# Last expert pairs in another order, the last w2 by column halves, and the final norm by halves on three engines

## The chip, the cores and the metric

The kernel runs on one core of one Trainium2 chip. The core has five engines with queues of their own: TensorE (PE), VectorE (DVE), ScalarE (ACT), GpSimd (POOL) and SyncE (SP), which here only issues transfers. They meet at semaphores. The metric is the device time of one execution in microseconds (us), the median of several runs.

## The reference, cut to what matters

One block of a hybrid encoder over 512 tokens of width 1024 in f32: two kinds of attention, cross attention to 256 memory tokens, then a mixture of 32 experts in 4 groups, of which every token takes two, and a last norm. The change touches the experts and the last norm:

```python
def expert_block(args):
    tok, gte, e = args
    xb = x_pad[tok]
    hb = jax.nn.silu(xb @ w1[e]) * (xb @ w3[e])
    return (hb @ w2[e]) * gte[:, None].astype(x2.dtype)
...
y = jnp.zeros((n + 1, d), x2.dtype).at[slot_tok].add(y_slots.reshape(n_slots, d))
...
h = h + y_f.reshape(b, s, d)
return rms_norm(h, final_norm)      # h / sqrt(mean(h*h) + 1e-6) * final_norm
```

w1 and w3 are (1024, 512) for each expert and w2 is (512, 1024).

## The kernel before, in words

The first half of the kernel does norms, projections and attention. From about 540 us on it works through the 32 experts in 16 pairs (`NPAIR`), p = 0 to 15. Each expert has a block of up to 64 tokens (`BLK`), so a pair fills 128 rows. What more tokens an expert has is done by loops at the end (`n_over`); the trace has no row of them, so these inputs do not need them.

For a pair, G = x w1 and U = x w3 are summed in two PSUM banks, ScalarE forms sigmoid(G) (`sg`), VectorE gg = G sg and then Hs = gg · gate · U. TensorE transposes Hs (`turn_hidden`), ScalarE copies the result out of PSUM to `HT` (`hidden`), and TensorE forms Y = H w2 in PSUM banks 4 and 5, 512 columns each (`down`). ScalarE copies Y to `Yh` (`output`), VectorE keeps the rest, `Yl` = Y - Yh (`rest`), and TensorE brings the rows of the pair back to their tokens by products with a 0/1 matrix `S` (`combine`, eight tiles of 128 tokens x 512 columns, two products each). VectorE adds these eight tiles to `h` (`add_one`).

Weights come as parts c of an expert: 0 and 1 are the halves of w1, 2 and 3 of w3, 4 and 5 of w2, 1 MB each. `SEQ_W` is the order in which TensorE uses them; a load is issued by SP when the place that it takes, one of nine in the ring `eraw`, was used (`e_wused`). `take_place` builds the list `LOADS` from that order. So the order of the loads and the order of the products come from one table. In it G of a pair stands ahead of w2 of the pair before: while TensorE does G of pair p, VectorE and ScalarE make Hs and HT of pair p-1.

The last pair has its own forms: `last_up` does U in two column halves (banks `U_BANK`), so that Hs, the transposes (`turn_last`) and HT (`last_hidden`) go by halves too; its w2 rows are laid out so that part 4 needs only the first half of HT. Both parts cover all 1024 columns. The sums of pair 14 are cut in two (`combine_half`), one ahead of U's second half and one between the two last transposes.

The last norm: ScalarE forms the sum of squares of each of four token tiles (128 x 1024), VectorE from these the inverse root (`inverse_root`: mean, ScalarE's square root, one over it, and one Newton step) for tiles 0 and 1, then for 2 and 3 (`step`). Tiles 0, 2 and 3 are scaled by VectorE in one product with the root and `gain_o`, tile 1 (`OUT_ACT`) by ScalarE (root) and GpSimd (gain). SP stores tiles in the order 0, 2, 1, 3.

Of the kernel before, what the change touches and what calls it, by code (L numbers as in the profile page):

```python
# [6 lines left out]
D = 1024  # L7
# [3 lines left out]
TT = SEQ // P  # L11
# [10 lines left out]
NE = NG * EPG  # L22
DE = 512
BLK = 64
# [17 lines left out]
def build(nc, x, mem, mix_norm, w_in, lam_q1, lam_k1, lam_q2, lam_k2, diff_subln, w_branch_a, w_branch_b,  # L42
# [486 lines left out]
    over_read = sem("over_read")  # L529
    u_half, out_by_root, out_rooted, out_done = (sem(n) for n in ("u_half", "out_by_root", "out_rooted", "out_done"))  # L530
# [62 lines left out]
    def take_place(parts):  # L593

        slot = took[0] % NS
        took[0] += 1
        for e, c, n, start in parts:
            free_at = max([LAST_OF.get((slot, start + WCH * i), 0) for i in range(n)])
            LOADS.append((slot, start, e, c, n, free_at))
# [25 lines left out]
    LAST_COMB = [(0, 0), (1, 0), (0, 1), (1, 1), (2, 0), (2, 1), (3, 0), (3, 1)]  # L625
# [3 lines left out]
    OUT_ACT = 1  # L629
    LAST_BANK = [6, 3, 1, 2, 0, 7, 4, 5]  # L630
# [27 lines left out]
    def place_view(slot, start, c, n):  # L658
        return eraw[slot][:, start:start + WCH * n].rearrange("p (k n) -> p k n", n=512 if c < 4 else D)

    block = nc.Block()
    with block:
# [3 lines left out]
        def _(sp):  # L666
# [17 lines left out]
            def load_expert(n):  # L684
                slot, start, e, c, halves, _ = LOADS[n]
                sp.dma_start(place_view(slot, start, c, halves), expert_src(e, c, halves)).then_inc(e_loaded[slot], 16)
# [69 lines left out]
        def _(pool):  # L756
# [82 lines left out]
            pool.wait_ge(out_rooted, 2)  # L839
            pool.wait_ge(out_by_root, 1)  # L840
            pool.tensor_tensor(h[:, OUT_ACT, :], h[:, OUT_ACT, :], gain_o[:, :], ALU.mult).then_inc(out_scaled[OUT_ACT], 1)


        @block.scalar
        def _(act):
# [261 lines left out]
            def output(p):  # L1107

                if p:
                    act.wait_ge(comb_made, NC * p)  # L1110
                for n in (0, 1):
                    if n == 0:
                        act.wait_ge(y_half, p + 1)
                    else:
                        act.wait_ge(e_wused, both_used(p, 5))
                    act.activation(Yh[:, 512 * n:512 * n + 512], ps[4 + n][:, :], ACT.Copy).then_inc(yh_kept, 1)  # L1116

            rows_kept(0)
            for p in range(NPAIR):
                if p:  # L1120
                    hidden(p - 1)
                act.wait_ge(e_wused, both_used(p, 1))
# [3 lines left out]
                if p:  # L1126
                    output(p - 1)
# [32 lines left out]
            act.activation(sqr[:, 15:16], ident[:, 0:1], ACT.Sqrt)  # L1160
            for t in range(TT):
                act.wait_ge(comb_added, NC * (NPAIR - 1) + LAST_COMB.index((t, 1)) + 1)
                act.wait_ge(n_sum, SUM_UPTO["h2"] + t)
                act.activation(junk_t[:, :], h[:, t, :], ACT.Square, accum_out=ss[:, t:t + 1]).then_inc(n_sum, 1)
                if t % 2 == 1:
                    root("out", slice(t - 1, t + 1), t // 2)

            act.wait_ge(out_rooted, 1)
            act.activation(h[:, OUT_ACT, :], h[:, OUT_ACT, :], ACT.Copy, scale=rs[:, OUT_ACT:OUT_ACT + 1]).then_inc(out_by_root, 1)
# [3 lines left out]
        def _(dve):  # L1173
# [395 lines left out]
            def body(p):  # L1569

                dve.wait_ge(sg_done, p + 1)
                dve.tensor_tensor(gg[:, :], ps[1][:, :], sg[:, :], ALU.mult).then_inc(gg_done, 1)  # L1572
                if p:
                    rest(p - 1)
                if p + 1 < NPAIR:
                    rows_kept(p + 1)
                if p:
                    add_half(p - 1, 0)
                    if p + 1 < NPAIR:
                        add_half(p - 1, 1)  # L1580
# [16 lines left out]
                if p == NPAIR - 1:  # L1597
                    add_half(p - 1, 1)
# [67 lines left out]
            for step in (0, 1):  # L1666
                dve.wait_ge(n_sum, SUM_UPTO["h2"] + 2 * step + 2)
# [9 lines left out]
        def _(pe):  # L1677
# [360 lines left out]

            def turn_last(half):
# [15 lines left out]
            def down(p, c):  # L2055
# [3 lines left out]
                pe.wait_ge(ht_kept, p + 2 if (p, c) == (NPAIR - 1, 5) else p + 1)  # L2059
                if c == 4 and p:  # L2060
                    pe.wait_ge(comb_added, NC * p if p < NPAIR - 1 else NC * p - NC // 2)
# [27 lines left out]
            def body(p):  # L2089
                pe.wait_ge(xt_kept, 2 * p + 2)  # L2090
                if p:
# [22 lines left out]
                if p < NPAIR - 1:  # L2114
                    up(p, 2)
                else:
                    last_up(2)
                if p:
                    combine_half(p - 1, 0)
                if p == NPAIR - 1:  # L2120
                    last_up(3)
                    turn_last(0)

                    pe.wait_ge(gg_done, p + 1)
                    combine_half(p - 1, 1)
                    turn_last(1)
                    return
# [13 lines left out]
            down(NPAIR - 1, 4)  # L2141
            down(NPAIR - 1, 5)
# [72 lines left out]
```

## Time and profile before

| | us |
|---|---|
| median of 3 runs | 1037.38 (1037.16 to 1037.48) |
| the profiled execution | 1035.97 |
| its span | 1034.2 |
| TensorE busy | 986.9 (95%) |
| VectorE busy | 502.9 (49%) |
| ScalarE busy | 341.8 (33%) |
| GpSimd busy | 42.9 (4%) |
| expert weights (`eraw`), share of the last chain | 12% |

Times in the rows are counted from the start of the span. In the part with the experts TensorE is busy for 90% or more of nearly every slice of the page, and so are the DMA engines, which move 425 to 430 GB/s there. A row of the timeline or the chain puts like instructions together (x16 is sixteen of them); a product with f32 operands counts as two. In brackets stands the engine's idle time before it, and what ended it.

### The profile page before, as it was taken

The page shows a single profiled execution, that of the slowest core. Times are in us where ns is not written, and L with a number is a line of the kernel's source. Part 1 is how long each engine was busy: PE and PEld are TensorE (multiplying, and loading weights), DVE is VectorE, ACT ScalarE, POOL GpSimd, SP SyncE. Part 2 cuts the span into 40 slices and gives each one's busy share as a digit, 9 for nine tenths or more (in the row PEclk, how much of TensorE's full clock was granted, in tenths as well). Part 3 has the DMA queues.
Part 4 walks back from the last instruction along what each step waited for, and adds up shares of the span by engine and source line. Part 5 has one row for each costly group of instructions (what it writes and reads, how often), then busy time and mean ns, then how long its engine had stood idle before and what let it go on. Part 6 is the DMA issues. An engine that isn't in the chain of part 4 may idle for free.

```text
span 1034.2 us, 12625 instructions
## 1 busy us (share of the span) xinstructions
PE 986.9 (95%) x4909; PEld 624.6 (60%) x4909; DVE 502.9 (49%) x920; ACT 341.8 (33%) x685; POOL 42.9 (4%) x62
## 2 busy tenths in 40 slices
PE   8999999999999999999996999999999889898994
PEld 6778877867788898877785344444443333333342
DVE  5369799777466355433338133333332223333336
ACT  6332356767862354534233111111111110111113
POOL 1000000000000000000001000000000000000001
PEclk9999999999999999999998999999999999999998
DMA  8422222121123535313297999999999999999992
GB/s 237 136 82 82 90 74 82 41 82 42 42 82 135 192 122 174 125 69 122 65 389 293 408 430 424 427 427 425 428 425 427 429 427 426 427 425 425 420 415 113
DMA packets 65583, 260.72 MB, mean 252 GB/s; under 512 B 11457, under 2 KB 39154, under 8 KB 50930
## 3 DMA queue, kind: packets, MB, share of 16 engines
q1 hardware_dynamic: 61106, 248.08, 60.4%
q0 software_dynamic: 3392, 8.39, 2.2%
q10 hardware_dynamic: 1024, 3.41, 0.9%
q8 instruction: 41, 0.67, 0.3%
q14 instruction: 20, 0.16, 0.0%
HBM read 259.60 MB, written 4.19 MB: 255 GB/s over the span
## 4 chain that ended last, share of the span: by engine, by line
PE 74%; DMA 13%; DVE 5%; ACT 3%; issue 3%; DVEq 0%; ACTq 0%; SPq 0%; POOLq 0%
PE ps L2014 16%; PE ps L1694 12%; DMA eraw<-in_w 12%; PE ps L1696 12%; PE ps L1695 12%; PE ps L2067 8%; PE ps L2078 2%; PE ps L2079 2%; PE ps L1929 1%; PE ps L1951 1%; PE ps L1871 1%; PE ps L2001 1%; DVE s L1306 1%; DVE nmax L1308 1%; PE ps L2052 1%
## 5 line engine op out<-in xcount | busy, mean ns | idle before, releaser
L2014 PE MATMUL ps<-eraw,XT 128*64 128x512 f32 x992 | 226.0, 598 | 10.8 <-DMA eraw<-in_w 9.6
L1257 DVE TENSOR_TENSOR wlo<-raw,whi 128x2048 fp32r<-128x2048 f32 (+2 forms) x43 | 95.9, 2230 | 117.3 <-ACT whi L939 117.2
L2014 PEld LDWEIGHTS ps<-eraw,XT 128*64 128x64 f32 x992 | 67.2, 136 | 131.9 <-issue 127.6
L2067 PE MATMUL ps<-eraw,HT 128*64 128x512 f32 x512 | 112.9, 593 | 7.8 <-issue 7.8
L1563 DVE TENSOR_TENSOR h<-ps,h 128x512 f32<-128x512 f32 x128 | 79.4, 684 | 81.6 <-PE ps L2079 81.6
L1694 PE MATMUL ps<-xT_hi,whi 128*128 128x512 f32 (+1 forms) x256 | 103.8, 405 | 1.3 <-DVE xT_lo L1264 1.3
L1696 PE MATMUL ps<-xT_hi,wlo 128*128 128x512 f32 (+1 forms) x256 | 100.2, 392 | 0.0
L1695 PE MATMUL ps<-xT_lo,whi 128*128 128x512 f32 (+1 forms) x256 | 100.0, 391 | 0.0
L939 ACT ACTIVATE whi<-raw 128x2048 fp32r<-128x2048 f32 (+2 forms) x43 | 80.2, 1866 | 45.4 <-PE ps L1696 45.4
L2067 PEld LDWEIGHTS ps<-eraw,HT 128*64 128x64 f32 x512 | 38.7, 137 | 79.8 <-issue 79.2
L1097 ACT ACTIVATE HT<-ps 128x512 f32<-128x512 f32 x15 | 9.0, 597 | 195.7 <-PE ps L2052 195.7
L1555 DVE TENSOR_TENSOR Yl<-ps,Yh 128x512 fp32r<-128x512 f32 x32 | 22.1, 692 | 96.2 <-ACT Yh L1116 96.2
L1694 PEld LDWEIGHTS ps<-xT_hi,whi 128*128 128x128 f32 (+1 forms) x256 | 47.7, 186 | 20.2 <-issue 8.9
L1572 DVE TENSOR_TENSOR gg<-ps,sg 128x512 f32<-128x512 f32 x16 | 11.1, 692 | 96.5 <-ACT sg L1125 94.5
L1696 PEld LDWEIGHTS ps<-xT_hi,wlo 128*128 128x128 f32 (+1 forms) x256 | 47.7, 186 | 10.9
L2078 PE MATMUL ps<-Yh,S 128*128 128x512 f32 x128 | 53.7, 419 | 0.4 <-issue 0.4
L1695 PEld LDWEIGHTS ps<-xT_lo,whi 128*128 128x128 f32 (+1 forms) x256 | 47.8, 187 | 9.4
L1116 ACT ACTIVATE Yh<-ps 128x512 fp32r<-128x512 f32 x32 | 19.1, 597 | 100.2 <-PE ps L2067 100.2
L2079 PE MATMUL ps<-Yl,S 128*128 128x512 f32 x128 | 50.4, 394 | 0.0
L2078 PEld LDWEIGHTS ps<-Yh,S 128*128 128x128 f32 x128 | 24.0, 187 | 28.9 <-issue 24.4
L1011 ACT ACTIVATE s<-s,nmax 128x128 f32<-128x128 f32 (+3 forms) x64 | 35.4, 559 | 1.1 <-DVE nmax L1308 1.0
L1125 ACT ACTIVATE sg<-ps 128x512 f32<-128x512 f32 x16 | 9.6, 597 | 77.0 <-PE ps L2014 77.0
(325 smaller groups left out, 1563.4 us busy)
## 6 DMA issues: line engine op xcount, KB each, us to landing
eraw<-in_w SPq DMA_DIRECT2D x74, 2048.0 KB, 27.7
eraw<-in_w SPq DMA_DIRECT2D x44, 1024.0 KB, 25.8
raw<-in_w_in SPq DMA_DIRECT2D x9, 1024.0 KB, 5.0
raw<-in_w_gate SPq DMA_DIRECT2D x8, 1024.0 KB, 5.4
raw<-in_w_ckv SPq DMA_DIRECT2D x8, 1024.0 KB, 5.3
raw<-in_w_out SPq DMA_DIRECT2D x4, 1024.0 KB, 5.1
raw<-in_w_cq SPq DMA_DIRECT2D x4, 1024.0 KB, 5.0
raw<-in_w_co SPq DMA_DIRECT2D x4, 1024.0 KB, 5.0
```

The lines of the kernel that those rows point to most:

```text
L939: act.activation(whi[n % 2][:, 0:w], raw[n % RING][:, 0:w], ACT.Copy).then_inc(w_hi, 1)
L1011: act.activation(b, b, ACT.Exp, bias=nmax[:, u % 3, m:m + 1], accum_out=ssum[:, u % 3, m:m + 1]).then_inc(exp_done, 1)
L1257: dve.tensor_tensor(wlo[n % 2][:, 0:w], raw[n % RING][:, 0:w], whi[n % 2][:, 0:w].bitcast(f32), ALU.subtract).then_inc(w_lo, 1)
L1555: dve.tensor_tensor(Yl[:, c], ps[4 + n][:, :], Yh[:, c].bitcast(f32), ALU.subtract).then_inc(yl_kept, 1)
L1563: dve.tensor_tensor(v, ps[bank][:, :], v, ALU.add).then_inc(comb_added, 1)
L1694: pe.matmul(o, ahi, bhi, start=start, stop=False)
L1695: pe.matmul(o, ahi, blo, start=False, stop=False)
L1696: return pe.matmul(o, alo, bhi, start=False, stop=stop)
L2014: ins = pe.matmul(ps[1 + c // 2][rows, :], XT[p % 2][:, kk, rows], eraw[slot][:, first + 512 * k:first + 512 * k + 512], start=(kk == 0), ...
L2067: ins = pe.matmul(ps[4 + n][rows, :], HT[:, ff, rows], eraw[slot][:, first + D * f + 512 * n:first + D * f + 512 * n + 512], start=(ff == ...
L2078: pe.matmul(o, S[:, P * t:P * t + P], Yh[:, c], start=True, stop=False)
L2079: pe.matmul(o, S[:, P * t:P * t + P], Yl[:, c], start=False, stop=True).then_inc(comb_made, 1)
```

## The change

It has three parts.

1. In `SEQ_W`, and in the code of TensorE, ScalarE and VectorE, w2 of pair 14 comes ahead of G of pair 15. Both halves of the sums of pair 14 now stand ahead of U's second half, and the two last transposes directly behind it.
2. w2 of the last pair is loaded and used by column halves: part 4 is columns 0 to 511 of all 512 rows and part 5 columns 512 to 1023, the latter in two pieces of two row groups with a semaphore for each. Rows of 4 KB in the load become rows of 2 KB. `last_down` replaces `down` for this pair.
3. The eight last tiles are summed in the order of their columns (first 0 to 511 of all tokens, `LAST_COMB`). Each addition is followed by a square of that half on ScalarE; VectorE adds the two sums. Of every tile VectorE scales columns 512 to 1023, while columns 0 to 511 are multiplied by the gain on GpSimd, as soon as their squares are taken, and then by the root on ScalarE. Stores go in the order 0 to 3.

```diff
-        for q, c in ((p, 0), (p, 1), (p - 1, 4), (p - 1, 5), (p, 2), (p, 3)):
+        ahead, behind = [(p, 0), (p, 1)], [(p - 1, 4), (p - 1, 5)]
+        for q, c in (behind + ahead if p == NPAIR - 1 else ahead + behind) + [(p, 2), (p, 3)]:
...
-    def take_place(parts):
+    def take_place(parts, pieces=(None,)):
...
-                take_place([(e, c + half, 1, 0), (e + 1, c + half, 1, WCH)])
+                take_place([(e, c + half, 1, 0), (e + 1, c + half, 1, WCH)],
+                           [slice(0, 2), slice(2, 4)] if (e, c + half) == (NE - 2, 5) else [None])
...
-    LAST_COMB = [(0, 0), (1, 0), (0, 1), (1, 1), (2, 0), (2, 1), (3, 0), (3, 1)]
+    LAST_COMB = [(t, n) for n in (0, 1) for t in range(TT)]
...
-            v = w2v_last
+            return w2v_last[e, :, :, 512 * (c - 4):512 * (c - 4) + 512]
...
 sync:
-            for t in (0, 2, 1, 3):
-                sp.wait_ge(out_scaled[t], 1)
+            for t in range(TT):
+                sp.wait_ge(out_scaled[t], 2)
...
 gpsimd:
-            pool.wait_ge(out_rooted, 2)
-            pool.wait_ge(out_by_root, 1)
-            pool.tensor_tensor(h[:, OUT_ACT, :], h[:, OUT_ACT, :], gain_o[:, :], ALU.mult).then_inc(out_scaled[OUT_ACT], 1)
+            for t in range(TT):
+                pool.wait_ge(out_sum, t + 1)
+                pool.tensor_tensor(h[:, t, 0:512], h[:, t, 0:512], gain_o[:, 0:512], ALU.mult).then_inc(gained, 1)
...
 scalar:
+            for j, (t, n) in enumerate(LAST_COMB):
+                act.wait_ge(comb_added, NC * (NPAIR - 1) + j + 1)
+                if j >= 2:
+                    act.wait_ge(out_sum, j - 1)
+                act.activation(junk_t[:, 512 * (j % 2):512 * (j % 2) + 512], h[:, t, 512 * n:512 * n + 512], ACT.Square,
+                               accum_out=ss[:, TT * n + t:TT * n + t + 1]).then_inc(out_sum, 1)
+                if j == NC - 2:
+                    root("out", slice(0, 2), 0)
+            root("out", slice(2, 4), 1)
+
             for t in range(TT):
...
+                act.wait_ge(out_rooted, t // 2 + 1)
+                act.wait_ge(gained, t + 1)
+                act.activation(h[:, t, 0:512], h[:, t, 0:512], ACT.Copy, scale=rs[:, t:t + 1]).then_inc(out_scaled[t], 1)
...
 vector:
+                if name == "out":
+                    link(dve.tensor_tensor(ss[:, c], ss[:, c], ss[:, TT + c.start:TT + c.stop], ALU.add))
...
                 for t in (2 * step, 2 * step + 1):
-                    if t != OUT_ACT:
-                        dve.scalar_tensor_tensor(h[:, t, :], h[:, t, :], rs[:, t:t + 1], gain_o[:, :],
-                                                 ALU.mult, ALU.mult).then_inc(out_scaled[t], 1)
+                    dve.scalar_tensor_tensor(h[:, t, 512:], h[:, t, 512:], rs[:, t:t + 1], gain_o[:, 512:],
+                                             ALU.mult, ALU.mult).then_inc(out_scaled[t], 1)
...
 tensor:
+            def last_down(n):
+                p = NPAIR - 1
+                at_ = [PLACE[2 * p + m, 4 + n] for m in (0, 1)]
+                pe.wait_ge(comb_added, NC * p - NC // 2)
+                for ff in range(4):
+                    if n == 0 and ff == 0:
+                        for slot, _, upto in at_:
+                            pe.wait_ge(e_loaded[slot], upto)
+                    elif n == 1 and ff % 2 == 0:
+                        pe.wait_ge(last_loaded[ff // 2], 32)
+                    pe.wait_ge(ht_kept, p + 1 + ff // 2)
+                    for m, (slot, first, _) in enumerate(at_):
...
             def body(p):
                 pe.wait_ge(xt_kept, 2 * p + 2)
+                if p == NPAIR - 1:
+                    turn_hidden(p - 1)
+                    down(p - 1, 4)
+                    down(p - 1, 5)
+                    pe.wait_ge(gg_done, p)
+                    up(p, 0)
+                    up(p, 1)
+                    combine_half(p - 1, 0)
+                    last_up(2)
+                    pe.wait_ge(gg_done, p + 1)
+                    combine_half(p - 1, 1)
+                    last_up(3)
+                    turn_last(0)
+                    turn_last(1)
+                    return
```

On TensorE, where pair 14 meets pair 15, the order before was (XT_110 are the tokens of pair 14 and XT_111 those of pair 15; eraw_62 to eraw_64 and eraw_56 to eraw_59 are places of the ring; `ident,Hs` are transposes, `eraw,HT` is w2; this list counts a product once):

```order
L2014 MATMUL ps<-eraw_62,XT_110 64x512 x4
L2014 MATMUL ps<-eraw_63,XT_111 64x512 x4
L2052 MATMUL ps<-ident,Hs 128x128 x4
L2014 MATMUL ps<-eraw_63,XT_111 64x512 x4
L2014 MATMUL ps<-eraw_64,XT_111 64x512 x8
L2067 MATMUL ps<-eraw_56,HT 64x512 x8
L2067 MATMUL ps<-eraw_57,HT 64x512 x8
L2031 MATMUL ps<-eraw_58,XT_111 64x256 x16
L2078 MATMUL ps<-Yh,S 128x512
```

and it is now, in the same place:

```order
L2031 MATMUL ps<-eraw_62,XT_110 64x512 x4
L2087 MATMUL ps<-ident,Hs 128x128 x4
L2102 MATMUL ps<-eraw_63,HT 64x512 x8
L2102 MATMUL ps<-eraw_64,HT 64x512 x8
L2031 MATMUL ps<-eraw_56,XT_111 64x512 x8
L2031 MATMUL ps<-eraw_57,XT_111 64x512 x8
L2113 MATMUL ps<-Yh,S 128x512
L2114 MATMUL ps<-Yl,S 128x512
```

The transposes moved from the middle of G to directly behind the last product of pair 14's U, w2 moved ahead of G, and the first half of the sums moved from behind U's first half to directly behind G.

On TensorE behind U's second half of the last pair the order before was:

```order
L2031 MATMUL ps<-eraw_59,XT_111 64x256 x16
L2043 MATMUL ps<-ident,Hs 128x128 x2
L2078 MATMUL ps<-Yh,S 128x512
L2079 MATMUL ps<-Yl,S 128x512
L2078 MATMUL ps<-Yh,S 128x512
L2079 MATMUL ps<-Yl,S 128x512
L2078 MATMUL ps<-Yh,S 128x512
L2079 MATMUL ps<-Yl,S 128x512
L2078 MATMUL ps<-Yh,S 128x512
L2079 MATMUL ps<-Yl,S 128x512
L2043 MATMUL ps<-ident,Hs 128x128 x2
L2140 TENSOR_LOAD over_i
```

and now it is (`eraw_60` and `eraw_61` hold the two parts of the last w2):

```order
L2113 MATMUL ps<-Yh,S 128x512
L2114 MATMUL ps<-Yl,S 128x512
L2048 MATMUL ps<-eraw_59,XT_111 64x256 x16
L2078 MATMUL ps<-ident,Hs 128x128 x4
L2179 TENSOR_LOAD over_i
L2179 ISA x2
L2069 MATMUL ps<-eraw_60,HT 64x512 x8
L2069 MATMUL ps<-eraw_61,HT 64x512 x8
```

The sums no longer stand between the two pairs of transposes.

On ScalarE the end of the kernel was (`ss` are the sums of squares, `sqr<-vv` the square roots):

```order
L1160 ACT_TABLE_LOAD
L1160 ACTIVATE sqr<-ident 128x1
L1164 ACTIVATE junk_t,ss<-h 128x1024 x2
L861 ACTIVATE sqr<-vv 128x2
L1164 ACTIVATE junk_t,ss<-h 128x1024 x2
L861 ACTIVATE sqr<-vv 128x2
L1169 ACTIVATE h<-h,rs 128x1024
```

and is now:

```order
L1172 ACT_TABLE_LOAD
L1172 ACTIVATE sqr<-ident 128x1
L1177 ACTIVATE junk_t,ss<-h 128x512 x7
L869 ACTIVATE sqr<-vv 128x2
L1177 ACTIVATE junk_t,ss<-h 128x512
L869 ACTIVATE sqr<-vv 128x2
L1186 ACTIVATE h<-h,rs 128x512 x4
```

Both roots stand ahead of all four scalings.

## Rows read from the trace of the kernel before

**Rows 1.** The chain that ended last, in order of time: start us, us, what
```profile
970.38 26.66 DMA eraw<-in_w
...
1027.67 3.28 DVEq L662
```

**Rows 2.** Windows: busy PE, PEld, DVE, ACT, POOL; PEclk, DMA share, GB/s
```profile
970.40:996.40 26.00, 26.00 (x118) 9.95 (x116) 9.24 (x15) 2.93 (x7) 0.00 (x0) 1.00 1.01 422
```

**Rows 3.** Timeline, last pairs: start us, us, engine, line, op, [idle before]
```profile
979.99 3.65 PE L2014 MATMUL ps<-eraw,XT 128*64 128x512 f32 x16
...
982.09 0.75 DVE L1586 SCALAR_TENSOR_TENSOR Hs<-gg,pair_gates,ps 128x512 f32<-128x512 f32 x1 [0.89 <-PE ps L2014]
...
983.57 0.75 PE L2052 MATMUL ps<-ident,Hs 128*128 128x128 f32 x4
...
984.36 0.60 ACT L1097 ACTIVATE HT<-ps 128x512 f32<-128x512 f32 x1 [12.66 <-PE ps L2052]
...
989.45 7.04 PE L2067 MATMUL ps<-eraw,HT 128*64 128x512 f32 x32
...
997.18 3.67 PE L2031 MATMUL ps<-eraw,XT 128*64 128x256 f32 x32 [0.69 <-DMA eraw<-in_w]
...
1006.42 0.44 PE L2043 MATMUL ps<-ident,Hs 128*128 128x128 f32 x2
1006.57 0.48 DVE L1595 SCALAR_TENSOR_TENSOR Hs<-gg,pair_gates,ps 128x256 f32<-128x256 f32 x1 [1.17 <-PE ps L2031]
1006.62 0.48 PE L2078 MATMUL ps<-Yh,S 128*128 128x512 f32 x1
...
1008.55 0.38 PE L2043 MATMUL ps<-ident,Hs 128*128 128x128 f32 x2
1008.87 7.09 PE L2067 MATMUL ps<-eraw,HT 128*64 128x512 f32 x32
```

**Rows 4.** Line L686, the last load alone: issue, and time to landing
```profile
L686 SPq DMA_DIRECT2D eraw<-in_w x1: 4312/4312/4312, 990.3 to 990.3; - x1
...
DMA to landing us min/median/max: 21.9/21.9/21.9
```

**Rows 5.** Windows: a w_out load, last w2 loads, last stores
```profile
294.50:295.00 0.50, 0.50 (x4) 0.42 (x3) 0.00 (x0) 0.50 (x2) 0.00 (x0) 1.00 1.05 410
1004.00:1005.00 1.00, 1.00 (x12) 0.67 (x10) 0.13 (x2) 0.00 (x0) 0.00 (x0) 1.00 1.03 410
1032.00:1032.50 0.50, 0.00 (x0) 0.00 (x0) 0.00 (x0) 0.00 (x0) 0.00 (x0) 0.50 1.01 410
```

**Rows 6.** Timeline behind the last products, VectorE and ScalarE
```profile
1017.33 4.88 DVE L1563 TENSOR_TENSOR h<-ps,h 128x512 f32<-128x512 f32 x8
...
1017.93 0.20 ACT L1160 ACTIVATE sqr<-ident 128x1 f32<-128x1 f32 x1
...
1022.12 0.16 DVE L1200 TENSOR_SCALAR vv<-ss 128x2 f32<-128x2 f32 x1
...
1022.55 0.17 DVE L1202 RECIPROCAL rs<-sqr 128x2 f32<-128x2 f32 x1 [0.27 <-ACT sqr L861]
...
1023.65 1.28 DVE L1672 SCALAR_TENSOR_TENSOR h<-h,rs,gain_o 128x1024 f32<-128x1024 f32 x1
```

**Rows 7.** Timeline of ScalarE, two exponentials with a running sum
```profile
270.44 0.71 ACT L1011 ACTIVATE s<-s,nmax 128x512 f32<-128x512 f32 x1
...
271.14 0.71 ACT L1011 ACTIVATE s<-s,nmax 128x512 f32<-128x512 f32 x1
```

**Rows 8.** Line L1672, its three products: count, durations ns, first and last start
```profile
L1672 DVE SCALAR_TENSOR_TENSOR h<-h,rs,gain_o x3: 1283/1284/3360, 1023.7 to 1027.6; 128x1024 f32<-128x1024 f32 x3
```

**Rows 9.** Timeline of GpSimd's product in the tail
```profile
1026.44 3.42 POOL L841 TENSOR_TENSOR h<-h,gain_o 128x1024 f32<-128x1024 f32 x1 [83.34 <-DVEq L1669]
```

**Rows 10.** Line L751, the four stores: issues, and time to landing
```profile
L751 SPq DMA_DIRECT2D out<-h x4: 332/344/369, 1025.0 to 1031.0; - x4
...
DMA to landing us min/median/max: 2.6/2.6/2.8
```

More of the change, by code:

```diff
@@ L529, in build @@
     over_read = sem("over_read")
+    last_loaded = [sem(f"last_loaded{i}") for i in (0, 1)]
+    out_sum, gained = sem("out_sum"), sem("gained")
     u_half, out_by_root, out_rooted, out_done = (sem(n) for n in ("u_half", "out_by_root", "out_rooted", "out_done"))
@@ L591, in build @@
     took = [0]
-    def take_place(parts):
+    def take_place(parts, pieces=(None,)):
         slot = took[0] % NS
         took[0] += 1
-        for e, c, n, start in parts:
-            free_at = max([LAST_OF.get((slot, start + WCH * i), 0) for i in range(n)])
-            LOADS.append((slot, start, e, c, n, free_at))
+        for rows in pieces:
+            for e, c, n, start in parts:
+                free_at = max([LAST_OF.get((slot, start + WCH * i), 0) for i in range(n)])
+                LOADS.append((slot, start, e, c, n, rows, free_at))
         upto = 16 * sum(load[0] == slot for load in LOADS)
@@ L656, in hidden_tile, with place_view @@
         return slice(P * ff, P * ff + P) if p == NPAIR - 1 else slice(ff, DE, 4)
-    def place_view(slot, start, c, n):
-        return eraw[slot][:, start:start + WCH * n].rearrange("p (k n) -> p k n", n=512 if c < 4 else D)
+    def place_view(slot, start, c, n, by_columns=False):
+        return eraw[slot][:, start:start + WCH * n].rearrange("p (k n) -> p k n", n=512 if c < 4 or by_columns else D)
     block = nc.Block()
@@ L684, in load_expert @@
             def load_expert(n):
-                slot, start, e, c, halves, _ = LOADS[n]
-                sp.dma_start(place_view(slot, start, c, halves), expert_src(e, c, halves)).then_inc(e_loaded[slot], 16)
+                slot, start, e, c, halves, rows, _ = LOADS[n]
+                last_w2 = c >= 4 and e // 2 == NPAIR - 1
+                dst, src = place_view(slot, start, c, halves, last_w2), expert_src(e, c, halves)
+                if rows is not None:
+                    dst, src = dst[:, rows], src[:, rows]
+                sp.dma_start(dst, src).then_inc(last_loaded[rows.start // 2] if last_w2 and c == 5 else e_loaded[slot], 16)
             def load_place(slot):
@@ L1111, in output @@
                 for n in (0, 1):
-                    if n == 0:
+                    if p == NPAIR - 1:
+                        act.wait_ge(e_wused, both_used(p, 4 + n))
+                    elif n == 0:
                         act.wait_ge(y_half, p + 1)
@@ L1121, in _ @@
                     hidden(p - 1)
+                if p == NPAIR - 1:
+                    output(p - 1)
                 act.wait_ge(e_wused, both_used(p, 1))
@@ L1125, in _ @@
                 act.activation(sg[:, :], ps[1][:, :], ACT.Sigmoid).then_inc(sg_done, 1)
-                if p:
+                if 0 < p < NPAIR - 1:
                     output(p - 1)
@@ L1160, in _ @@
             act.activation(sqr[:, 15:16], ident[:, 0:1], ACT.Sqrt)
-            for t in range(TT):
[L1162 to L1169, printed above, removed]
+            for j, (t, n) in enumerate(LAST_COMB):
[7 more added lines that the diff above has]
+            root("out", slice(2, 4), 1)
+            for t in range(TT):
+                act.wait_ge(out_rooted, t // 2 + 1)
+                act.wait_ge(gained, t + 1)
+                act.activation(h[:, t, 0:512], h[:, t, 0:512], ACT.Copy, scale=rs[:, t:t + 1]).then_inc(out_scaled[t], 1)
         @block.vector
@@ L1569, in body @@
             def body(p):
+                if p == NPAIR - 1:
+                    rest(p - 1)
                 dve.wait_ge(sg_done, p + 1)
                 dve.tensor_tensor(gg[:, :], ps[1][:, :], sg[:, :], ALU.mult).then_inc(gg_done, 1)
-                if p:
+                if 0 < p < NPAIR - 1:
                     rest(p - 1)
@@ L1578, in body @@
                     add_half(p - 1, 0)
-                    if p + 1 < NPAIR:
-                        add_half(p - 1, 1)
+                    add_half(p - 1, 1)
                 dve.wait_ge(gg_done, p + 1)
@@ L1666, in _ @@
             for step in (0, 1):
-                dve.wait_ge(n_sum, SUM_UPTO["h2"] + 2 * step + 2)
+                dve.wait_ge(out_sum, NC // 2 + 2 * step + 2)
                 inverse_root("out", D, slice(2 * step, 2 * step + 2), step)
@@ L2037, in last_up @@
                                 ins.then_inc(u_half, 1)
+            def last_down(n):
[10 more added lines that the diff above has]
+                    for m, (slot, first, _) in enumerate(at_):
+                        rows = slice(BLK * m, BLK * m + BLK)
+                        ins = pe.matmul(ps[4 + n][rows, :], HT[:, ff, rows], eraw[slot][:, first + 512 * ff:first + 512 * ff + 512],
+                                        start=(ff == 0), stop=(ff == 3))
+                        if ff == 3:
+                            ins.then_inc(e_wused, 1)
             def turn_last(half):
@@ L2058, in down @@
                     pe.wait_ge(e_loaded[slot], upto)
-                pe.wait_ge(ht_kept, p + 2 if (p, c) == (NPAIR - 1, 5) else p + 1)
+                pe.wait_ge(ht_kept, p + 1)
                 if c == 4 and p:
-                    pe.wait_ge(comb_added, NC * p if p < NPAIR - 1 else NC * p - NC // 2)
+                    pe.wait_ge(comb_added, NC * p)
                 for n, f in [(0, 0), (1, 0), (0, 1), (1, 1)] if c == 4 else [(0, 0), (0, 1), (1, 0), (1, 1)]:
@@ L2090, in body @@
                 pe.wait_ge(xt_kept, 2 * p + 2)
+                if p == NPAIR - 1:
+                    turn_hidden(p - 1)
[12 more added lines that the diff above has]
+                    return
                 if p:
@@ L2113, in body @@
                     pe.wait_ge(h_done, p)
[L2114 to L2117, printed above, removed]
+                up(p, 2)
                 if p:
                     combine_half(p - 1, 0)
[L2120 to L2127, printed above, removed]
                 up(p, 3, (0, 1))
@@ L2140, in _ @@
             n_over = pe.value_load(over_i[0:1, 0:1], min_val=0, max_val=MAX_OVER)
-            down(NPAIR - 1, 4)
-            down(NPAIR - 1, 5)
+            last_down(0)
+            last_down(1)
             with pe.If(n_over > 0):
```

5 lines of the change are left out of this document (1 added, 4 removed).

## The prediction, written before the run

> **What bounds the kernel now.** I read the chain of waits from its end first. Its last long wait for data is a piece 26.66 us long that starts at 970.38 and ends at 997.04 [rows 1]: the first half of U's weights (w3) of the last pair of experts. Before it the stream of expert weights sets the pace, and behind it no transfer stands in the chain. Next I asked what TensorE did meanwhile. The windows show it busy for 26.00 of 26.00 us from 970.4 to 996.4, at a granted clock of 1.00, with the DMA engines full too, at 422 GB/s [rows 2]. So in the last 26 us before that wait both are full, and the wait that names the DMA cost TensorE 0.69 us, no more [rows 3]. That is the point of my argument: the stream can be rearranged, but the work of TensorE behind it has no slack. Then I read the order of TensorE's work for the last two pairs in the timeline [rows 3]. Sixteen pieces start at 979.99 (the trace counts each product as two); eight of them end U of pair 14, the other eight begin G of pair 15. While these run, VectorE makes Hs from 982.09 to 982.84, so the transposes at 983.57 find it ready, and while ScalarE copies HT (984.36, 0.60 us) TensorE goes on with G. No product waits. w2 of pair 14 follows at 989.45, U of pair 15 at 997.18, and w2 of pair 15 from 1008.87 for 7.09 us, to 1015.96. I call that end E; the span's end at 1034.2 is E+18.24. The last load lands at 990.3 + 21.9 = 1012.2 [rows 4].
>
> The profiled execution took 1035.97 us, its span 1034.2, so 1.8 us lie around it. The median of the timed runs is 1037.38, 1.4 us above the profiled one. I work the change out within the span and add it to the median.
>
> **The last pairs, part by part.** Nothing changes before the end of U of pair 14, eight pieces into the group at 979.99, at 979.99 + (983.57 - 979.99)/2 = 981.78. The loads are issued behind the same waits, and each pair of loads takes the place that another one had.
> - The idle time of 0.69 us before 997.18 goes. U's first half now starts behind G and one half of the sums of pair 14, about 1000.5 (984.35 below, plus 7.05 for w2, 7.16 for G's 32 pieces at the same pace, and 2.0 for the sums), when its weights have been there since 997.04. That is -0.69.
> - The transposes of pair 14 now stand right behind the last product that Hs needs. Hs starts at 982.09 and takes 0.75, the transposes can start at 982.9, HT starts 0.79 behind them as now (983.57 to 984.36), ends at 984.3, and w2 starts at 984.35. From 981.78 that is 2.57 us, of which the transposes are 0.7: TensorE idles for 1.87 that G of pair 15 now covers. From below, Hs and HT could not be quicker than their 0.75 and 0.60, so 1.4 is the least; 2.3 if each handover costs 0.1 more. I take +1.87.
> - The second half of the sums moves ahead of U's second half, so that nothing covers the last transposes. Now 2.45 us lie between the first of them (1006.42) and w2 (1008.87), 1.93 of them sums (1006.62 to 1008.55). Then the second Hs (starts 0.15 behind, takes 0.48) lets the second transposes start at 0.65, and w2 starts 0.32 later (1008.55 to 1008.87), at 0.97; the sums cost their 1.93, and some 0.1 of a fresh start, elsewhere. 0.97 + 2.03 - 2.45 = +0.55; at least +0.3.
> - w2 of the last pair by column halves has the same 32 pieces, 7.09 us. The halves of its last data are wanted when its columns 512 to 1023 start, some 3.5 us before the new end, and 1.8 before it. With the new end near 1017.7 these are 1014.1 and 1015.9, against 1012.2 now. The rows of 4 KB become 2 KB: the stream's rate with 4 KB rows is 410 GB/s, and a load of w_out, which has 2 KB rows, also runs at 410 [rows 5]. Were it 5% less, the last 4 MB would be 0.5 us late, and 1.9 us of slack hide that. SP's two additional DMAs wait behind a full queue, but the next thing SP waits for comes ten microseconds later. I cost this at nothing, gain included: the first half of Y is ready early, but TensorE has no place to use it before its last product.
>
> Sum for TensorE: -0.69 + 1.87 + 0.55 = +1.73. The new end E is 1017.7.
>
> **Sums, squares and scaling.** All counted from E. The first addition starts at E+1.37 and eight take 4.88, to E+6.25, as now [rows 6]; the order of the columns does not change that.
> - The squares start when the square root's table is in, at E+2.2 (1017.93 + 0.20). Two exponentials of 512 columns with a running sum follow each other in 0.70 us (270.44, 271.14) [rows 7]; six squares at 0.70 are read out by E+6.4 to 6.5. So they keep up with the additions.
> - GpSimd now multiplies four halves while VectorE adds. The one multiplication of 1024 columns is recorded at 3.42 us, but VectorE's product started at the same time as it took its usual 1.28, and the next one took 3.36 [rows 8, 9]. So they took turns: GpSimd held VectorE up for 3.36 - 1.28 = 2.08. Half of it is 1.04 a half tile; 1.71 from the recorded span is the upper bound. Four from E+3.0 end at E+7.2 (at most E+9.8). The new addition of two sums on VectorE would start at E+6.5; it reads SBUF twice, as the held-up product did, and I let it wait until E+7.2. The Trainium skill, page "SBUF — State Buffer", section "🔬 SBUF: two separate sides", says that a VectorE operation with two SBUF inputs and a GpSimd operation that reads SBUF exclude each other for the whole instruction. By that rule the trace agrees (3.36 against 1.28), and the running additions, with one input in PSUM, would not be held.
> - Then ss ready E+7.4, mean E+7.56 (0.16 each), root E+7.8, Newton's steps 1.10 (1022.55 to 1023.65), so scaling starts at E+8.95. Two half tiles take 1.4 (0.75 for one of 512, some 0.65 behind another) to E+10.35. Only then does VectorE form the second mean, 0.43 (1022.12 to 1022.55) plus 0.2 for the sum: E+10.98.
> - ScalarE is held by its own order: its second root stands ahead of all its scalings. So tiles 0 and 1 are scaled at E+11.0 to 12.15 (0.60 each), tiles 2 and 3 by E+12.75 and 13.4. The first store goes at E+11.6. It now goes at 1025.0, which is E+9.0.
> - Four stores of 512 KB then follow within 1.9 us. One lands 2.6 us after its issue [rows 10]; at 410 GB/s its bytes are 1.28 of that. Four one behind the other: 2.6 - 1.28 + 5.12 = 6.44 after the first issue, E+18.05. Behind the last landing (1031.0 + 2.8 = 1033.8) stand 0.4 us now: E+18.45. Now it is E+18.24, so this part gives +0.2 at my values. Squares at 0.63 or an addition that isn't held give -0.7; GpSimd at 1.71 gives +2.6 at most. The stall of 2.08 in VectorE's last product goes, and 1.3 us of stores that now lie ahead of the others come to lie behind them.
>
> Total +1.73 + 0.2 = +1.9: 1037.38 + 1.9 = 1039.3.
>
> **Rivals.**
> 1. The additions are held by GpSimd too. No row shows a GpSimd operation that reads SBUF beside an addition out of PSUM. If each of the four multiplications takes a turn of 1.04 from E+3.2 on, the eighth addition ends at E+10.4, not 6.25, and the mean starts there instead of at E+7.2: 3.2 more, +5.1, 1042.5. It decides from the second turn on, since one turn is hidden behind the squares. Against it: the rule above. Chance 12%.
> 2. The stream, not TensorE, sets the end. Then w2 ends 1.77 (eight of its 32 pieces) behind the last landing, 1012.2 + 1.77 = 1014.0, not 1017.7: 1014.0 is 1.96 before 1015.96, and with +0.2 that gives 1035.6, or 1034.7 with the second part at its -0.7. For it: the chain names the DMA up to 997.04. Against it: 26.00 of 26.00 us busy. Chance 7%. It would be on the fast side, and only just.
> 3. The stores do not queue behind each other, so the last one alone counts: E+13.4 + 0.1 + 2.8 + 0.4 = E+16.7, 1.5 less than now; +1.73 - 1.5 gives 1037.6. Against it: the stores alone reach the 410 GB/s that the weights reach too [rows 5], so each fills all the engines. Chance 5%.
>
> **The numbers.** My forecast holds 76%, at 1037.9 to 1040.6: TensorE's terms can be 0.5 less (bubble 1.4, last transposes 0.3) or 0.4 more, the second part -0.7 to +0.9 before the extremes. About 0.2%, 2.07 us, is what a measurement can tell from no change; the forecast of +1.9 lies just inside. So I give it 42% of its weight as slower and 58% within: 0.32 and 0.44. Rival 1 adds 0.12 to slower, rival 2 gives 0.05 to faster and 0.02 to within, rival 3 0.05 to within. Together faster 0.05, within 0.51, slower 0.44. The range reaches towards rival 2 and up to rival 1: 1036.4 to 1042.4.
>
> **What would show it.** TensorE idle for about 1 us on each side of the transposes at 983, w2 of pair 14 at 984.4, no wait for eraw behind 981, its last product at 1017.7. U's first half starting at 1000.5. If w2 of pair 14 starts before 983.7, or the last product ends before 1016.5, my sum is wrong in its first part. VectorE's additions still 0.61 apart; if 1.6 apart, rival 1. The addition of ss between E+6.5 and E+7.4. ScalarE's first scaling behind its second root, near E+11; the four stores issued within 2 us. A first store before E+10 would make the second part wrong.

## The result, and the profile after

| | before, us | after, us |
|---|---|---|
| median | 1037.43 (8 runs, 1036.56 to 1038.06) | 1041.91 (8 runs, 1038.89 to 1042.78) |
| profiled execution / its span | 1035.97 / 1034.2 | 1042.65 / 1040.9 |
| A, start of the last eight pieces of U of pair 14 | 979.99 | 981.80 |
| E, end of w2 of pair 15 | 1015.96 (A+35.97) | 1022.10 (A+40.30) |
| span's end | E+18.24 | E+18.80 |

After takes 1.0042 of the time of before, interval 1.0033 to 1.0052: +4.5 us, slower. The predicted +1.9 was on the right side of nothing, and too small by more than half. That A itself lies 1.81 later does not come from the change: the seven kernels with the new order had A from 979.42 to 981.80, the five with the old one from 979.99 to 981.85, and up to A they all do the same work. What differs is TensorE's granted clock much earlier: in a pause of 5.7 us at 548 it falls to 0.50 in every trace, and stays there for 6.8 us in before and for 10.2 us in after. So I count from A to E and from E to the end: +4.33 and +0.56.

TensorE's rows of after for the last two pairs (the timeline; columns as in [rows 3]), with the two copies and Hs:

```profile
981.80 1.94 PE L2031 MATMUL ps<-eraw,XT 128*64 128x512 f32 x8
...
983.91 0.75 DVE L1606 SCALAR_TENSOR_TENSOR Hs<-gg,pair_gates,ps 128x512 f32<-128x512 f32 x1 [0.89 <-PE ps L2031]
...
984.75 0.72 PE L2087 MATMUL ps<-ident,Hs 128*128 128x128 f32 x4 [1.02 <-issue]
...
985.51 0.60 ACT L1105 ACTIVATE HT<-ps 128x512 f32<-128x512 f32 x1 [12.00 <-PE ps L2087]
...
986.37 8.78 PE L2102 MATMUL ps<-eraw,HT 128*64 128x512 f32 x32 [0.89 <-ACT HT L1105]
...
994.95 7.06 PE L2031 MATMUL ps<-eraw,XT 128*64 128x512 f32 x32
...
1004.01 3.67 PE L2048 MATMUL ps<-eraw,XT 128*64 128x256 f32 x32
...
1009.66 3.67 PE L2048 MATMUL ps<-eraw,XT 128*64 128x256 f32 x32
...
1013.26 0.44 PE L2078 MATMUL ps<-ident,Hs 128*128 128x128 f32 x2
...
1013.94 0.44 PE L2078 MATMUL ps<-ident,Hs 128*128 128x128 f32 x2 [0.24 <-DVE Hs L1615]
1014.32 0.75 DVE L1567 SCALAR_TENSOR_TENSOR S<-slot_row,pair_slots,S 128x512 fp32r<-128x512 f32 x1
1014.42 0.38 ACT L1111 ACTIVATE HT<-ps 128x256 f32<-128x256 f32 x1 [0.29 <-PE ps L2078]
```

The transposes have a gap on each side, 1.02 and 0.89, where [rows 3] has none. And w2 of pair 14, 32 pieces as before, takes 8.78 where it took 7.04. The windows of after say why (busy of TensorE, PEclk, DMA share, GB/s):

```profile
985.00:986.00 1.00, 0.48 (x4) 1.00 1.02 426
986.00:987.00 1.00, 0.64 (x2) 0.77 1.00 418
987.00:988.00 1.00, 1.00 (x5) 0.50 0.98 410
988.00:989.00 1.00, 1.00 (x6) 0.50 1.02 426
989.00:990.00 1.00, 1.00 (x5) 0.53 1.02 426
990.00:991.00 1.00, 1.00 (x6) 1.00 1.02 426
```

For 3.4 us (986.5 to 989.9, by the shares in the windows) TensorE runs at a granted clock of 0.50, its 1.2 GHz level, just as w2 begins, and then it is back at 1.00, 2.4 GHz. It takes windows of a microsecond or two to see this; a slice of the page's clock row is 26 us long.

TensorE's waits of after, from 981 to 1023 (total, times, longest), name no transfer; in [rows 3] one stood there:

```profile
PE ps L2087 <- issue: 1.0, 1, 1.0
PE ps L2102 <- ACT HT L1105: 0.9, 1, 0.9
PE ps L2069 <- ACT HT L1111: 0.6, 1, 0.6
PE ps L2078 <- DVE Hs L1615: 0.2, 1, 0.2
```

The tail of after, VectorE, ScalarE and GpSimd:

```profile
1023.45 4.88 DVE L1582 TENSOR_TENSOR h<-ps,h 128x512 f32<-128x512 f32 x8
...
1024.17 0.63 ACT L1177 ACTIVATE junk_t<-h 128x512 f32<-128x512 f32 x1
...
1024.80 0.62 ACT L1177 ACTIVATE junk_t<-h 128x512 f32<-128x512 f32 x1
1024.98 4.97 POOL L849 TENSOR_TENSOR h<-h,gain_o 128x512 f32<-128x512 f32 x4 [80.67 <-ACT junk_t L1177]
...
1028.24 0.51 DVE L1218 TENSOR_TENSOR ss<-ss 128x2 f32<-128x2 f32 x1
...
1028.78 1.20 DVE L1219 TENSOR_SCALAR vv<-ss 128x2 f32<-128x2 f32 x1
...
1031.35 1.41 DVE L1689 SCALAR_TENSOR_TENSOR h<-h,rs,gain_o 128x512 f32<-128x512 f32 x2
...
1033.18 2.54 ACT L1186 ACTIVATE h<-h,rs 128x512 f32<-128x512 f32 x4
```

The additions are where they were, E+1.35 for 4.88 [rows 6], though GpSimd works beside them. The mean (`vv`), two columns wide, takes 1.20 where [rows 6] has 0.16. The stores by their line, to be read against [rows 10]:

```profile
L759 SPq DMA_DIRECT2D out<-h x4: 356/384/980, 1033.9 to 1035.9; - x4
...
DMA to landing us min/median/max: 2.7/3.7/4.6
```

They are issued within 2.0 us and take from 2.7 up to 4.6 us to land, where [rows 10] has 2.6 to 2.8: they queue.

### The profile page after: what moved, and what is told of

Same layout as the page of the kernel before. It is cut to its first block, busy times and chain, and to the rows that moved or that the text cites. A ratio compares the mean times of both kernels' runs of the same rounds, so it can differ in the third digit from the quotient of the medians.

```text
span 1040.9 us, 12648 instructions
## 1 busy us (share of the span) xinstructions
PE 990.6 (95%) x4909; PEld 627.1 (60%) x4909; DVE 501.5 (48%) x923; ACT 343.8 (33%) x696; POOL 44.5 (4%) x65
## 4 chain that ended last, share of the span: by engine, by line
PE 82%; DMA 10%; ACT 3%; DVE 2%; issue 2%; ACTq 0%; DVEq 0%
PE ps L2031 17%; PE ps L1711 13%; PE ps L1713 13%; PE ps L1712 13%; DMA eraw<-in_w 9%; PE ps L2102 8%; PE ps L2113 3%; PE ps L2114 2%; PE ps L1888 2%; PE ps L1946 1%; PE ps L1968 1%; PE ps L2018 1%; PE ps L1896 1%; PE ps L1909 1%; PE ps L2087 1%
## 5 line engine op out<-in xcount | busy, mean ns | idle before, releaser
L2102 PE MATMUL ps<-eraw,HT 128*64 128x512 f32 x480 | 107.6, 601 | 8.8 <-issue 7.8
```

The lines of the kernel that those rows point to most:

```text
L2102: ins = pe.matmul(ps[4 + n][rows, :], HT[:, ff, rows], eraw[slot][:, first + D * f + 512 * n:first + D * f + 512 * n + 512], start=(ff == ...
```

## The experiments

Each was compared with the kernel before in runs on the same chip. My theory at this point: after is slower by the order of the last pairs (two gaps, and the clock that they cost), a little by the norm, and not at all by the column halves. The rival: each part costs some, or the columns and their 2 KB rows slow the stream.

**The order alone.** The changes to `SEQ_W` and to the code of TensorE, ScalarE and VectorE for pair 14, nothing else:

```diff
+            if p == NPAIR - 1:
+                turn_hidden(p - 1)
+                down(p - 1, 4)
+                down(p - 1, 5)
```

> Only the first part: w2 of pair 14 ahead of G of pair 15, both halves of pair 14's sums ahead of U's second half, the last transposes together; last w2 and the norm as before. Theory (TensorE's order is the cost): TensorE stands for 1.0 us on either side of pair 14's transposes, its granted clock then falls to half for some 3.5 us and w2 of pair 14 takes 8.8 instead of 7.05, and the last w2 starts 1 us later behind the last transposes; +3.5 to +4.6 us against before. Rival (the stream or the norm is the cost): under +1.5 us.

Measured: 1040.49 (6 runs) against 1036.52, ratio 1.0031 (1.0019 to 1.0043). A to E is 40.28, +4.31, the tail 18.28. Both gaps and the slow w2 are there:

```profile
983.80 0.72 PE L2056 MATMUL ps<-ident,Hs 128*128 128x128 f32 x4 [1.02 <-issue]
...
985.41 8.78 PE L2071 MATMUL ps<-eraw,HT 128*64 128x512 f32 x32 [0.89 <-ACT HT L1100]
```

So the order holds all of TensorE's loss, and some nine tenths of the whole in the traces.

**The norm alone.** `LAST_COMB`, the squares and scalings by halves, and the stores' order:

```diff
-    LAST_COMB = [(0, 0), (1, 0), (0, 1), (1, 1), (2, 0), (2, 1), (3, 0), (3, 1)]
+    LAST_COMB = [(t, n) for n in (0, 1) for t in range(TT)]
```

> Only the third part: sums, squares and scaling by halves on three engines; the order and the last w2 as before. Theory: the end of TensorE stays, and behind it 18.8 us instead of 18.24, because the second mean waits for GpSimd's fourth product and the four stores go within 2 us; +0.3 to +0.9 us. Rival (the additions or the norm carry the loss): +2 us or more, additions of VectorE over 0.61 us apart.

Measured: 1037.12 (12 runs) against 1036.52, ratio 1.0002 (0.9994 to 1.0011). In the trace the tail is 18.79, +0.55, the same as in after; that is less than the timing can tell from nothing.

**The column halves alone.** `last_down` for the last pair, and its loads:

```diff
-            down(NPAIR - 1, 4)
-            down(NPAIR - 1, 5)
+            last_down(0)
+            last_down(1)
```

> Only the second part: the last w2 loaded and used by column halves, in rows of 2 KB; the order and the norm as before. Theory: nothing, -0.3 to +0.4 us, since TensorE uses each half later than it lands. Rival (2 KB rows slow the stream): the last loads land 1 us or more later and w2's second half waits, +1 us or more.

Measured: 1036.73 (11 runs) against 1036.52, ratio 0.9999 (0.9990 to 1.0008); A to E 35.98, tail 18.26. Nothing, as costed. The 2 KB rows cost the end nothing.

**Is it the gaps that cost the clock?** After, with useless products of 128x256 put in both, four ahead of pair 14's transposes and three behind:

```diff
+                    for _ in range(4):
+                        pe.matmul(ps[7][:, 0:256], ident[:, :], gain_o[:, 0:256], start=True, stop=True)
                     turn_hidden(p - 1)
+                    for _ in range(3):
+                        pe.matmul(ps[7][:, 0:256], ident[:, :], gain_o[:, 0:256], start=True, stop=True)
```

> The changed kernel with seven products without use (128x256, to an idle bank) in the two gaps at pair 14's transposes, four ahead of them and three behind. Theory (the idle time lowers the granted clock): the clock stays 1.00 there, w2 of pair 14 takes 7.05 us instead of 8.8, the gaps themselves stay 1.0 and 0.9 us long; 1.2 to 2.0 us faster than the changed kernel, +2.5 to +3.3 against before. Rival (w2 is slowed by something else, its data or its copy): no change against the changed kernel, +4.5.

Measured: 1040.97 (6 runs), ratio 1.0040 (1.0027 to 1.0054). The clock is 1.00 from 980 to 992 and w2 takes 7.09, but it starts at A+5.56 and not A+4.57: a filler takes 0.46 there, in all a microsecond more than the gaps held. A to E is 39.57, 0.73 less than in after, and not the 1.2 to 2.0 that I had expected. That the gaps cost the clock is shown; more than half of the gain is given back, and the medians do not resolve the rest. Two and two should fit.

**What holds w2 of the last pair?** From the last transposes to w2 [rows 3] has 0.32 us; after has 1.07, though half of HT is enough to start. Between them in program order stands the read of a register, unchanged by the diff. In this run it is moved ahead of the last pieces of U:

```diff
                     last_up(2)
                     pe.wait_ge(gg_done, p + 1)
                     combine_half(p - 1, 1)
+                    n_over_of.append(pe.value_load(over_i[0:1, 0:1], min_val=0, max_val=MAX_OVER))
...
-            n_over = pe.value_load(over_i[0:1, 0:1], min_val=0, max_val=MAX_OVER)
+            n_over = n_over_of[0]
```

> The changed kernel; TensorE's queue reads the count of overflowing experts (a register load) ahead of U's second half instead of between the last transposes and the last w2. Theory (that load stands open once no sums cover it): the last w2 starts 1.0 us behind the first of the last transposes instead of 1.75, 0.6 to 0.8 us faster than the changed kernel's 40.30 us from U of pair 14 to TensorE's end. Rival (w2 waits for HT's second half): 1.75 us and the same time.

Measured: 1041.21 (5 runs) against 1037.03, ratio 1.0038 (1.0024 to 1.0051). The medians cannot show 0.7 us; the rows do. The timeline has

```profile
1013.10 0.44 PE L2078 MATMUL ps<-ident,Hs 128*128 128x128 f32 x2 [0.24 <-DVE Hs L1615]
1013.46 0.20 PEld L2069 LDWEIGHTS ps<-eraw,HT 128*64 128x64 f32 x4 [0.17 <-issue]
1013.47 7.09 PE L2069 MATMUL ps<-eraw,HT 128*64 128x512 f32 x32
1013.48 0.75 DVE L1567 SCALAR_TENSOR_TENSOR S<-slot_row,pair_slots,S 128x512 fp32r<-128x512 f32 x1
1013.57 0.39 ACT L1111 ACTIVATE HT<-ps 128x256 f32<-128x256 f32 x1 [0.29 <-PE ps L2078]
```

w2 starts 0.37 behind the last transposes and ahead of the second copy of HT, which the wait table of after had named as its releaser. A to E is 39.57, 0.73 less. Here the releaser that the profile names was wrong: it is the last event that came, not the one waited for.

**Both together, with two and two fillers.**

```diff
+                    for _ in range(2):
+                        pe.matmul(ps[7][:, 0:256], ident[:, :], gain_o[:, 0:256], start=True, stop=True)
                     turn_hidden(p - 1)
+                    for _ in range(2):
+                        pe.matmul(ps[7][:, 0:256], ident[:, :], gain_o[:, 0:256], start=True, stop=True)
```

> The same early register load, and products without use in pair 14's two gaps, two in each (four and three were too many: they ended 1.0 us late). Theory: granted clock 1.00 throughout, w2 of pair 14 follows U's end as late as in the changed kernel, and takes 7 us: 37.8 to 38.2 us from U of pair 14 to TensorE's end instead of 40.30 (before: 35.97), +2.2 to +2.9 us against before. Rival (idle time is needed for the clock to fall, so little filling does nothing): clock at half again, 39.6.

Measured: 1038.74 (11 runs) against 1037.03, ratio 1.0020 (1.0011 to 1.0029). w2 of pair 14 starts at A+4.55, as in after, and takes 7.09:

```profile
983.97 7.09 PE L2102 MATMUL ps<-eraw,HT 128*64 128x512 f32 x32
```

A to E is 37.85, 2.45 less than after and 1.88 more than before. What is left is close to the cost of the order that I had predicted, +1.73.

**Which gap?** The same kernel with the fillers in one gap only.

> This is the kernel after with the register read ahead of the last piece of U, and two useless products ahead of pair 14's transposes, none behind them. It asks which of TensorE's two gaps, the 1.02 us ahead of the transposes or the 0.89 us behind them, costs the granted clock. Theory 1, only both together lower the clock: w2 of pair 14 runs at a granted clock of 1.00 and takes 7.09 us, from the start of U's last piece group to the end of w2 of pair 15 it is 37.85 us. Theory 2, a gap of 0.9 us is enough by itself: w2 of pair 14 takes 8.78 us, with the clock near 0.5 for some 3.5 us of it, and the stretch is 39.55 us. Speaking for theory 1: the kernel before has idle stretches of 0.69 to 0.81 us next to TensorE's last products and its clock stays at 1.00 there.

> The same, with the two useless products behind pair 14's transposes only; the 1.02 us ahead of them stays. Theory 1, only both gaps together lower the clock: 7.09 us for w2 of pair 14 and 37.85 us for the stretch. Theory 2, a gap of 1.02 us is enough by itself: 8.78 us, a clock near 0.5 for some 3.5 us, and 39.55 us.

Measured, one execution each: w2 of pair 14 takes 7.09 in both, A to E is 37.86 and 37.89. The clock holds with either gap left open:

```profile
984.11 7.09 PE L2102 MATMUL ps<-eraw,HT 128*64 128x512 f32 x32 [0.89 <-ACT HT L1105]
```

```profile
982.98 0.72 PE L2087 MATMUL ps<-ident,Hs 128*128 128x128 f32 x4 [1.02 <-issue]
983.54 1.03 PE L2129 MATMUL ps<-gain_o,ident 128*128 128x256 f32 x4
984.58 7.09 PE L2102 MATMUL ps<-eraw,HT 128*64 128x512 f32 x32
```

One execution each is thin, since the moment of a fall varies: in the pause at 548 the clock fell 1.5 to 4.4 us after TensorE's last product, depending on the execution. But the traces hold many more single gaps. From 785 to 978 TensorE stands idle twelve times in each of the twelve traces, for 0.98 to 1.86 us, some 10 to 20 us apart, and the clock stays at 1.00. In before, one of these gaps and the windows:

```profile
881.59 3.65 PE L2014 MATMUL ps<-eraw,XT 128*64 128x512 f32 x16 [1.66 <-DMA eraw<-in_w]
```

```profile
785.00:978.00 193.00, 175.56 (x799) 1.00 1.01 425
```

So a gap of 0.89 or 1.02 does not cost the clock by itself; the two together do, with 0.72 us of transposes between them, in three traces of three. A longer one may: in norm_only a gap of 2.02 us, from 14.5 to 16.5, has the clock at 0.50 right behind it, from 16.8 to 20.2, while before has 1.26 there and stays at 1.00.

```profile
16.50 0.50 PE L1701 MATMUL ps<-xT_hi,whi 128*128 128x512 f32 x1 [2.02 <-DVE xT_lo L1272]
```

```profile
17.00:20.00 3.00, 3.00 (x8) 0.50 1.07 345
```

One correction to what I wrote ahead of these two runs: of the idle stretches of 0.69 to 0.81 us, only the 0.69 is TensorE's own; 0.81 is idle time of its weight loads.

**Where the tail's half microsecond goes.** The kernel before with the norm by halves, but GpSimd multiplies only three of the four halves; VectorE scales tile 3 whole:

```diff
-            for t in range(TT):
+            for t in range(GAINED):
                 pool.wait_ge(out_sum, t + 1)
                 pool.tensor_tensor(h[:, t, 0:512], h[:, t, 0:512], gain_o[:, 0:512], ALU.mult).then_inc(gained, 1)
```

> The norm by halves alone, but GpSimd multiplies three half tiles, not four; VectorE scales tile 3 whole. Theory (GpSimd's products exclude VectorE's SBUF operations, not its additions out of PSUM): the mean behind the first sum takes 0.16 us instead of 1.2, the first store goes 1.1 to 1.3 us earlier and the end comes 17.4 to 17.8 us behind TensorE's end instead of 18.8; -0.4 to -1.0 us against before. Rival (the mean waits for something else, ScalarE's root or a semaphore): 1.2 us again, no difference to the norm by halves.

Measured: 1036.07 (11 runs) against 1037.03, ratio 0.9993 (0.9983 to 1.0002). The tail is 17.73, 1.06 less than with four.

```profile
1019.98 3.75 POOL L844 TENSOR_TENSOR h<-h,gain_o 128x512 f32<-128x512 f32 x3 [75.72 <-ACT junk_t L1168]
...
1023.24 0.51 DVE L1209 TENSOR_TENSOR ss<-ss 128x2 f32<-128x2 f32 x1
...
1023.78 0.17 DVE L1210 TENSOR_SCALAR vv<-ss 128x2 f32<-128x2 f32 x1
```

The mean is back at 0.17. The addition of `ss` ends at 1023.75, when GpSimd's third product does (1023.73): it is still held by that one. The second addition of this kind, with GpSimd done, takes 0.15 where this one takes 0.51.

**A version that beats both.** The last, with one inverse root for all four tiles in place of two, so that no second mean waits behind VectorE's scalings and no second root ahead of ScalarE's:

```diff
-            for step in (0, 1):
-                dve.wait_ge(out_sum, NC // 2 + 2 * step + 2)
-                inverse_root("out", D, slice(2 * step, 2 * step + 2), step)
+            for step in (0,):
+                dve.wait_ge(out_sum, NC)
+                inverse_root("out", D, slice(0, 4), step)
```

> Before with the norm by halves, three half tiles on GpSimd, and one inverse root for all four tiles behind the eighth square; the order of the experts and the last w2 as before. Theory: squares done 6.9 us behind TensorE's end, roots at 8.7, the first store at 9.5, then the four stores' own time: 16.1 to 16.6 us behind TensorE's end instead of 18.24; -1.6 to -2.2 us against before. Rival (the stores are not what bounds the end, VectorE's last product is): 15.5 to 16.0. Rival (holding tiles 0 and 1 back for tiles 2 and 3 costs what it saves): no difference.

Measured: 1035.26 (11 runs) against 1037.03, ratio 0.9984 (0.9975 to 0.9993), 1.8 us faster than before. A to E is 35.96 and the tail 16.59, 1.65 less than before. Of the 1.65, the halves with three products bring 0.51 (18.24 to 17.73) and the one root 1.14 (17.73 to 16.59), in one trace each; the medians do not tell these two shares apart. One root with the norm of before was not run. The root waits for all eight squares, at E+7.1, but the first store goes at E+9.7, 2.1 earlier than in after:

```profile
1025.20 0.16 DVE L1214 TENSOR_TENSOR rs<-rs,nw 128x4 f32<-128x4 f32 x1
1025.45 1.95 ACT L1175 ACTIVATE h<-h,rs 128x512 f32<-128x512 f32 x3 [1.09 <-DVEq L1677]
1025.51 3.27 DVE L1680 SCALAR_TENSOR_TENSOR h<-h,rs,gain_o 128x512 f32<-128x512 f32 x4
1026.29 2.91 SPq L754 DMA_DIRECT2D out<-h  x4
```

## Why the prediction was right and where it was wrong

| term | predicted | measured |
|---|---|---|
| idle ahead of U's first half | -0.69 | -0.84 |
| gaps around pair 14's transposes | +1.87 | +2.10 |
| last transposes uncovered | +0.55 | +0.64 |
| register read behind them | not in the sum | +0.70 |
| granted clock in w2 of pair 14 | not in the sum | +1.69 |
| column halves | 0 | 0 |
| tail | +0.2 | +0.56 |
| sum | +1.9 | +4.9 in the traces, +4.5 in the medians |

How the measured ones come out. Idle: from the start of w2 of pair 14 to the next block it is 6.89 with the gaps filled, against 7.73 in [rows 3]. Clock: 8.58 in after against that 6.89. Gaps: A to w2 is 4.57, less 1.79 for eight pieces and 0.68 for the transposes. Last transposes: 1.75 from the first of them to w2, plus 2.04 for the sums that moved (1007.62 to 1009.66), less 2.45 is 1.34; with the early read the 1.75 is 1.05, which splits it. The terms of TensorE make 4.29 of the 4.33; 0.04 is spread over the rest.

- **What bounds the kernel** held. TensorE had no slack behind the stream: with the changed order, but without the fall of the clock and the late register read, A to E grew by 1.88 against the predicted 1.73, and no product waited for a transfer. That it came so close is in part luck: the three terms were off by -0.15, +0.21 and +0.09.
- **The step that failed is the sum for TensorE.** It priced two gaps as idle time only, and every product behind them at its old duration. [Rows 2] show a granted clock of 1.00 with TensorE full, but [rows 5] show 0.50 at 1032, where it is idle, and I took nothing from that. The trace of before had the price too: the clock falls in the pause at 548, and when TensorE works again at 554.6 it does so at 0.50 until 557.8.

```profile
551.00:552.00 1.00, 0.00 (x0) 0.51 1.01 426
555.00:557.00 2.00, 2.00 (x9) 0.50 1.03 428
```

(The first product of an expert is at 566.0, and not near 540 as the description of the kernel has it.) A term with bounds was owed: nothing, as behind the single gaps of before, or half of those 3.2 us, 1.6 by estimate. It measured 1.69, over half of what was missing. The granted clock has two levels, set by how busy the engine has been lately, by the Trainium skill, page "TensorE: Matmul & The Clock Gate", section "🔬 Part 1: The HAM clock gate (the "warmup" mystery)". The trace agrees: 1.00 and 0.50, and the windows with 0.77 and 0.53 hold a change of level.
- **The last transposes** were priced nearly right as such (+0.55, +0.64). What I missed stands in the code and not in a row of before: a register read between them and w2. Before, the second transposes waited for nothing, so that TensorE's queue could run ahead of the array and do the read under the sums; after, the queue reaches it only once Hs has come. That the queue runs ahead is my reading; that the read costs 0.70 in this one place is shown.
- **The gaps** are 0.23 larger than taken: w2 starts 0.26 behind the copy of HT, not 0.05.
- **The tail**: the squares came faster than taken (0.62 apart, not 0.70), GpSimd's products slower (1.24, not 1.04, so to E+7.85 and not 7.2), and the wait was the one predicted, but for the mean too: VectorE got on at E+7.88. Everything behind is that 0.3 later: scaling E+9.25 (8.95), first store E+11.8 (11.6), end E+18.80 (18.45). I had expected the addition, which has two inputs in SBUF, to be held, and not the mean, which has one. The runs with three and four products show that GpSimd's fourth product holds the mean; that the addition is held rests on its end at the end of the third. The Trainium skill, page "SBUF — State Buffer", section "Who interferes with whom", says that a `tensor_scalar` can enter a mode of two ports, in which it contends with GpSimd. The trace agrees, 1.20 against 0.17 (that the mean ran in that mode is inferred), and the eight additions with one input in PSUM stayed 0.61 apart.
- **Rival 1** named 1042.5, next to the measured 1041.9, and is refuted all the same: additions 0.61 apart. Its number was met by accident. **Rival 2** (the stream sets the end): TensorE waited for no transfer from 981 on. **Rival 3** (stores don't queue): landings of 2.7 to 4.6.

The range held the time, near its upper end, because it reached for rival 1, not because the clock was in it. That is luck. The narrower stretch of the forecast, 1037.9 to 1040.6, missed it, and was summed up carelessly: its own terms, 1.4 instead of 1.87 and 0.3 instead of 0.55 below, 2.3 above, give 1037.7 to 1040.4. The signs that I gave for a wrong first part (w2 of pair 14 before 983.7, the last product before 1016.5) looked only to the early side, and the error was on the late one.

## What to carry to other kernels

Where a change makes a full TensorE wait, look at how the idle times lie together and price what its clock does to the work behind them: two gaps of about 1 us, one on each side of four transposes, cost nearly as much again as they held, and filling either with useless products got it back, while single gaps of up to 1.86 us, ten us or more apart, cost no clock. When the wait of a queue changes, list everything that stands between it and the next real instruction in program order, register reads included. In a tail of small dependent steps, count the rounds through other engines: in the traces, one root over four columns instead of two rounds over two brought 1.14 us, and the overlap of the halves 0.51.

## What the runs showed of the hardware

- TensorE's granted clock went to 0.50 for 3.4 us when gaps of 1.02 and 0.89 us lay around 0.72 us of transposes (three traces), and stayed at 1.00 with either of them filled (one trace each) and through single gaps of 0.98 to 1.86 us (twelve in each of twelve traces). In one pause of 5.7 us the fall came 1.5 to 4.4 us after the last product, depending on the execution.
- The read of a register on TensorE between the last transposes and w2 of the last pair cost 0.70 us.
- GpSimd's product of 128x512 took 1.26 to 1.29 us, with VectorE adding out of PSUM beside it; VectorE's operations on two columns ended only when it did: 1.20 us instead of 0.17 for the mean, with one input in SBUF, 0.51 instead of 0.15 for the addition, with two.
- A releaser in the wait table can be the wrong one: the read stood there as a wait for HT.
